# Moving the reload of a staging slot one store later on the GpSimd queue, in a one-core transformer and state-space kernel

## The chip, the core and the metric

The kernel runs on one core of a Trainium2 chip. A core has a matrix engine (TensorE, PE in the rows, with its weight loads as PEld), a vector engine (VectorE, DVE), an activation engine (ScalarE, ACT), GpSimd (POOL) and SyncE (SP). Each works through its own list of instructions in order and waits on semaphores for the others. Data moves between DRAM and the on-chip buffers by DMA; here SP, ACT and POOL issue DMAs. The metric is device time in microseconds (us) of one execution; lower is better.

## The reference

Two blocks run one after the other on 512 tokens of width 1024. Block one: an attention layer (eight stick-breaking heads, four differential heads), its output projection `w_o`, and a gated feed-forward. Block two: a wide input projection, a convolution branch, a bidirectional state-space scan, and 16 experts.

```python
x = x + mix @ w_o[layer]
h2 = rmsnorm(x, ffn_norm_g[layer])
x = x + (jax.nn.silu(h2 @ w_gate[layer]) * (h2 @ w_up[layer])) @ w_down[layer]
...
u = rms_norm(h, w_norm_mix[l])
proj = jnp.einsum('btd,dk->btk', u, w_in[l])
```

The change lies in the part of the program that covers these lines.

## The kernel before

Dense products of block one's feed-forward and of block two's projection are split products. A weight tile is written as a high part (a copy in the type `fp32r`, made by ACT) and a low part (tile minus high part, made by VectorE), and TensorE multiplies high by high, high by low and low by high.

The feed-forward has 76 such pieces. `FFT` is 22 (tiles of the hidden width), and the first 44 pieces are gate and up, two for each `m`; the other 32 are the down product, four for each of eight output tiles. `ffn_high(p)` (line 1314 and on) lets ACT make the high part of piece p in one of three buffers `WF`, as soon as TensorE has used piece p - 3; `ffn_low(p)` is VectorE's half of it. SP loads the raw weights into two slots of `ring`: 2 MB each for gate and up, 1.4 MB each for down, each issued when TensorE has finished the piece that last reads the slot.

Beside the feed-forward the kernel prepares the **72 weight tiles of the next projection** (`N_PROJ`, 512 KB each): their low parts are computed now and stored in DRAM, to be loaded again in the projection. Each tile q goes through a pipeline of four steps on three staging slots (`STAGE = 3`):

- POOL loads the raw tile into slot q % 3 of `arena` (`pre_load`, line 2303; DMA at line 2307, semaphore `pre_in`).
- ACT copies it as high part (`pre_high`, line 1328; instruction at line 1336). The high part goes to banks 6 and 7 of PSUM, of which there is one copy, so tile q waits for the low part of q - 1. The first `N_PRE_WO` tiles use `WF` instead, which is free until the feed-forward starts.
- VectorE subtracts and writes the low part to `PREL`, also three slots (`pre_low`, line 1854; instruction at line 1858).
- POOL stores it (line 2314, semaphore `pre_out`), after which both slots are free for tile q + 3.

Three tables say how many tiles are handled where in the lists of ACT and VectorE: `PRE_WO` for the eight output tiles of `w_o`, `PRE_GATE` for the 22 hidden tiles, `PRE_DOWN` for the eight output tiles of down. In the gate stage one tile of each `m` stands after `hidden_high(m - 1)` and the rest after `ffn_high(2m + 4)`; in the down stage they stand behind the four `ffn_high` of an output tile, and the square of the residual (`square("n3", ...)`) behind them. TensorE waits for the last of the 72 (`pe.wait_ge(S("pre_low"), N_PROJ)`) before the norm of the projection's input.

POOL's list here is one loop over q: wait for low part q, issue store q, and for q from 1 to 69 issue the load of tile q + 2, which needs store q - 1 to have landed.

Of the kernel before, what the change touches and what calls it, by code (L numbers as in the profile page):

```python
# [23 lines left out]
F32, F32R, U32 = mybir.dt.float32, mybir.dt.float32r, mybir.dt.uint32  # L24
# [15 lines left out]
FFT = FF // P  # L40
# [18 lines left out]
FBUF = 3  # L59
# [39 lines left out]
N_PROJ = len(PROJ)  # L99
STAGE = 3  # L100
PAIRS = 4
PRE_WO = [1, 2, 1, 2, 0, 0, 0, 0]
PRE_GATE = [2] * FFT
PRE_DOWN = [4, 3, 3, 3, 3, 3, 3, 0]
N_PRE_WO = sum(PRE_WO)
assert N_PRE_WO + sum(PRE_GATE) + sum(PRE_DOWN) == N_PROJ
FFN_W = 24
PROJ_W = FFN_W + 2 * FFT + 32
TAIL_W = PROJ_W + N_PROJ
# [33 lines left out]
def program(nc, inp, out):  # L143
    ctx = ExitStack()
    with ctx:
# [5 lines left out]
        def S(name):  # L151

            if name not in sems:
                sems[name] = ctx.enter_context(nc.semaphore(name))
            return sems[name]
# [19 lines left out]
        WF = ffn.enter_context(nc.sbuf_tensor("WF", [P, FBUF, PIECE], F32R))  # L175
# [60 lines left out]
        PS = ctx.enter_context(nc.psum_tensor("PS", [P, 8, 512], F32))  # L236
# [42 lines left out]


        _, ZSP, QK, V, MIX, ROPE = area([(P,), (5, 1280), (16, SEQ), (QB, D), (DT, SEQ), (2, SEQ)])

        SUMMED = U[:, 4, 0:3 * P]
# [43 lines left out]
        def pre_raw(q):  # L327
            return arena[:, PRE_AT + q % STAGE * PIECE:PRE_AT + q % STAGE * PIECE + PIECE]

        def pre_high_place(q):  # L330
            return PS[:, 6:8, :].rearrange("p a n -> p (a n)").bitcast(F32R) if q >= N_PRE_WO else WF[:, q % FBUF, :]

        def pair_of(p):
            return (p + 2) % PAIRS
# [49 lines left out]
        for b in range(2):  # L384
            block("out", (b,), (DT, 512))
        N_DENSE = len(loads)
        where = {name: n for n, (name, *_) in enumerate(loads)}

        slot_of, turn_, tail_turn = [], 0, 0
# [9 lines left out]
        for n, (name, *_) in enumerate(loads):  # L399
            count[slot_of[n]] += 16  # L400
            landed[name] = count[slot_of[n]]
# [90 lines left out]
        def freed(tag):  # L492
            b, n = order[tag]
            return S(f"freed{b}"), n

        def got(eng, tag):
            eng.wait_ge(*filled(tag))

        def free(ins, tag):
            return ins.then_inc(S(f"freed{order[tag][0]}"), 1)  # L500
# [657 lines left out]
        def _(act):  # L1158
# [3 lines left out]
            def square(nm, k, src, acc, T):  # L1162

                if k >= 3:
                    act.wait_ge(S("squares_added"), ADDS[nm] + k - 2)
                A(acc[:, 0:T] if k == 0 else SQ[:, k % 2, 0:T], src, ACT.Square).then_inc(S("sq_ready"), 1)
# [9 lines left out]
            def x_high(nm, k):  # L1176

                A(UX[:, 0, k, :], H[:, k, META:T2], ACT.Copy, scale=pcol(nm, k)).then_inc(S("x_high"), 1)
# [57 lines left out]
            for p in range(24):  # L1236
# [4 lines left out]
                if p - 2 in ROPE_AT:  # L1241
                    q = ROPE_AT.index(p - 2)
                    rope_root(2 * q)
                    rope_root(2 * q + 1)
                if p in ROPE_AT:
                    q = ROPE_AT.index(p)
# [19 lines left out]
            for n in range(DIFF_HEADS * QB + 3):  # L1266
# [14 lines left out]
                if 1 <= n <= DIFF_HEADS * QB:  # L1281
                    m = n - 1
# [6 lines left out]
                if n >= 3:  # L1289
                    m = n - 3  # L1290
# [23 lines left out]
            def ffn_high(p):  # L1314

                name = pieces[p][0]
                act.wait_ge(S(f"ring{slot_of[where[name]]}"), landed[name])
                if p >= FBUF:
                    act.wait_ge(*piece_used[p - FBUF])
                A(split_high(p), raw(p), ACT.Copy).then_inc(S("weights_high"), 1)  # L1320
# [7 lines left out]
            def pre_high(n):  # L1328

                for q in range(pre_turn[0], pre_turn[0] + n):  # L1330
                    act.wait_ge(S(f"pre_in{q % STAGE}"), 16 * (q // STAGE + 1))
                    if q >= N_PRE_WO:
                        act.wait_ge(S("pre_low"), q)
                    elif q >= FBUF:
                        act.wait_ge(S("pre_low"), q - FBUF + 1)
                    A(pre_high_place(q), pre_raw(q), ACT.Copy).then_inc(S("pre_high"), 1)  # L1336
                pre_turn[0] += n

            act.wait_ge(S("mix_ready"), DIFF_HEADS)
            for m in range(DT):  # L1340
                act.wait_ge(*freed(("wo", m)))
                x_high("ffn_g", m)
                square("n2", m, H[:, m, META:T2], RS, SEQ)
                pre_high(PRE_WO[m])
                if m == DT - FBUF - 1:
                    act.wait_ge(S("pre_low"), N_PRE_WO)
                if m >= DT - FBUF - 1 and m < DT - 1:
                    ffn_high(m - (DT - FBUF - 1))
            inverse_root("n2", (6,), SEQ)
            nc.scalar.preload_act_table_set("silu_and_others")  # L1350
            for m in range(FFT):
                ffn_high(2 * m + 3)
                if m >= 1:
                    hidden_high(m - 1)
                    pre_high(1)
                act.wait_ge(*freed(("ga", m)))
                A(SQ[:, m % 2, 0:SEQ], SQ[:, m % 2, 0:SEQ], ACT.Silu).then_inc(S("silu_ready"), 1)
                ffn_high(2 * m + 4)
                pre_high(PRE_GATE[m] - (m >= 1))
            nc.scalar.preload_act_table_set("natural_log_exp_and_others")  # L1360
# [342 lines left out]
        def _(dve):  # L1703
# [13 lines left out]
            def x_low(nm, k, base):  # L1717

                dve.wait_ge(S("x_high"), base + k + 1)
                V_.scalar_tensor_tensor(UX[:, 1, k, :], H[:, k, META:T2], pcol(nm, k), UX[:, 0, k, :].bitcast(F32), MUL, SUB)\  # L1720
                    .then_inc(S("x_low"), 1)

            def add_square(nm, k, acc, T):

                dve.wait_ge(S("sq_ready"), ADDS[nm] // (DT - 1) * DT + k + 1)
                if k >= 2:
                    dve.wait_ge(S("squares_added"), ADDS[nm] + k - 1)
                V_.tensor_tensor(acc[:, 0:T], acc[:, 0:T], SQ[:, k % 2, 0:T], ADD).then_inc(S("squares_added"), 1)
# [22 lines left out]
            for p in range(24):  # L1751
                b, m = divmod(p, 4)
# [19 lines left out]
                if p - 3 in ROPE_AT[:2]:  # L1772
                    q = ROPE_AT.index(p - 3)
# [34 lines left out]
            for n in range(DIFF_HEADS * QB + 2):  # L1808
# [11 lines left out]
                if n >= 2:  # L1820
                    m = n - 2
# [8 lines left out]
                if 1 <= n <= DIFF_HEADS * QB:  # L1830
                    m = n - 1
# [12 lines left out]
            def ffn_low(p):  # L1844
                dve.wait_ge(S("weights_high"), FFN_W + p + 1)
                V_.tensor_tensor(split_low(p), raw(p), split_high(p).bitcast(F32), SUB).then_inc(S("weights_low"), 1)  # L1846

            def hidden_low(m):
                dve.wait_ge(S("x_high"), GX_X + m + 1)
                V_.tensor_tensor(GX[:, 1, m, :], GXL[:, m, :], GX[:, 0, m, :].bitcast(F32), SUB).then_inc(S("x_low"), 1)  # L1850
# [3 lines left out]
            def pre_low(n):  # L1854

                for q in range(pre_turn[0], pre_turn[0] + n):
                    dve.wait_ge(S("pre_high"), q + 1)
                    V_.tensor_tensor(PREL[:, q % STAGE, :], pre_raw(q), pre_high_place(q).bitcast(F32), SUB).then_inc(S("pre_low"), 1)  # L1858
                pre_turn[0] += n

            for m in range(DT + 1):
                if m < DT:
                    got(dve, ("wo", m))
                    free(V_.tensor_tensor(H[:, m, META:T2], H[:, m, META:T2], PS[:, m % 4, :], ADD), ("wo", m))
                    dve.wait_ge(*freed(("wo", m)))
                if m >= 1:
                    x_low("ffn_g", m - 1, DT)
                    if m >= 2:
                        add_square("n2", m - 1, RS, SEQ)
                    pre_low(PRE_WO[m - 1])  # L1870
                if DT - FBUF <= m < DT:
                    ffn_low(m - (DT - FBUF))
            for m in range(FFT):
# [13 lines left out]
                ffn_low(2 * m + 4)  # L1887
                pre_low(PRE_GATE[m] - (m >= 1))
            hidden_low(FFT - 1)
# [105 lines left out]
            for g in range(GROUPS):  # L1995
# [18 lines left out]
                for s, c in enumerate(range(NC - 1, 0, -1)):  # L2014
                    t0, n = CHUNKS[c]
# [252 lines left out]
        def _(pool):  # L2268
# [34 lines left out]
            def pre_load(q):  # L2303

                if q >= STAGE:
                    pool.wait_ge(S(f"pre_out{q % STAGE}"), 16 * (q // STAGE))
                pool.dma_start(pre_raw(q), inp["w_proj"][q]).then_inc(S(f"pre_in{q % STAGE}"), 16)
# [4 lines left out]
            for q in range(N_PROJ):  # L2312
                pool.wait_ge(S("pre_low"), q + 1)
                pool.dma_start(low_dram[q], PREL[:, q % STAGE, :].bitcast(F32)).then_inc(S(f"pre_out{q % STAGE}"), 16)
                if 1 <= q <= N_PROJ - STAGE:
                    pre_load(q + STAGE - 1)

            pool.wait_ge(S("h_summed"), DT)
            pool.dma_start(h_dram, H[:, :, :]).then_inc(S("h_moved"), 16)
# [40 lines left out]
            for g in range(GROUPS):  # L2360
# [3 lines left out]
                for s, c in enumerate(range(NC - 1, 0, -1)):  # L2364
                    n = CHUNKS[c][1]
# [279 lines left out]
```

## Time and profile before

| | |
|---|---|
| median of 3 runs | 2706.44 us (2705.46 to 2711.19) |
| profiled execution, its own time | 2706.44 us |
| its span, first to last instruction | 2704.7 us |
| mean granted TensorE clock, share of full | 0.964 |
| PE busy | 2535.9 us (94%) |
| DVE busy / ACT busy / POOL busy | 1121.5 / 814.0 / 335.5 us |

The profile is one execution. Busy time counts what an engine executes; issuing a DMA is not counted as busy on the page, but a row of the timeline gives how long the issue took. In a timeline row the two numbers are start and duration, and the bracket says how long the engine was idle before it and who released it. For a DMA the profile knows the time from its issue to its landing. The stretch with which the change deals lies between 310 and 746 us of the span: the `w_o` product to 354.4 us, gate and up to 602.4 us, down to 726.2 us, then a norm and the start of block two's projection.

### The profile page before, as it was taken

What the parts mean: (1) busy time and instruction counts of PE and PEld (TensorE: products, weight loads), DVE (VectorE), ACT (ScalarE), POOL (GpSimd) and SP (SyncE); (2) the same over time, 40 slices, a digit from 0 to 9 for tenths busy, and PEclk for the clock granted to TensorE, in tenths of its full rate; (3) what the DMA queues carried; (4) which work ended last, traced back from release to release, by engine and by line L of the source; (5) the groups of instructions that cost most, each with busy time, mean ns of one, the idle gap of its engine ahead of it and who ended that gap; (6) DMA issues with size and microseconds to landing.
All of it is one profiled execution on the core that took longest, in us unless ns stands there. A gap on an engine that the chain in (4) does not pass through costs nothing.

```text
span 2704.7 us, 42580 instructions
## 1 busy us (share of the span) xinstructions
PE 2535.9 (94%) x18335; PEld 1583.1 (59%) x18335; DVE 1121.5 (41%) x1530; ACT 814.0 (30%) x1347; POOL 335.5 (12%) x411
## 2 busy tenths in 40 slices
PE   8998999999799898989779998999999999999996
PEld 6754478887589797979569973333333333333332
DVE  4336466653538878796965332111111111111111
ACT  3256454443345454544453221000000010000001
POOL 0033012111201212121520000000000000000000
PEclk9999999999989998999779999999999999999998
DMA  5100268885745454546432259999999999999993
GB/s 207 63 32 1 82 230 296 285 284 210 276 164 198 124 196 125 193 123 203 112 142 72 85 208 352 410 398 409 395 398 399 393 396 395 397 395 397 395 403 129
DMA packets 128630, 674.20 MB, mean 249 GB/s; under 512 B 19236, under 2 KB 52004, under 8 KB 99140
## 3 DMA queue, kind: packets, MB, share of 16 engines
q1 hardware_dynamic: 55584, 552.65, 52.5%
q0 software_dynamic: 25632, 88.49, 9.8%
q10 hardware_dynamic: 47236, 30.42, 4.1%
q8 instruction: 145, 2.38, 0.3%
q14 instruction: 33, 0.27, 0.0%
HBM read 617.47 MB, written 54.04 MB: 248 GB/s over the span
## 4 chain that ended last, share of the span: by engine, by line
PE 80%; DVE 12%; DMA 4%; ACT 2%; issue 2%; POOL 1%; ACTq 0%; POOLq 0%; DVEq 0%; SPq 0%
PE PS L1111 37%; PE PS L811 11%; PE PS L1013 4%; DVE H L1977 4%; PE PS L757 3%; PE PS L753 3%; PE PS L754 3%; DMA arena<-w_proj 2%; PE PS L1018 2%; PE PS L657 1%; PE PS L604 1%; PE PS L605 1%; PE PS L608 1%; PE PS L728 1%; PE PS L1101 1%
## 5 line engine op out<-in xcount | busy, mean ns | idle before, releaser
L1111 PE MATMUL PS<-expert_ring_low,U 128*32 128x512 f32 x4608 | 508.4, 593 | 0.9 <-DVE U L2219 0.9
L1111 PE MATMUL PS<-expert_ring_high,U 128*32 128x512 f32 x4608 | 504.8, 592 | 0.0
L811 PE MATMUL PS<-XH,RINGF 128*128 128x264 f32 x2304 | 400.0, 292 | 1.2 <-ACT arena L1428 1.2
L1111 PEld LDWEIGHTS PS<-expert_ring_high,U 128*32 128x32 f32 x4608 | 148.2, 110 | 336.7 <-issue 335.7
L1111 PEld LDWEIGHTS PS<-expert_ring_low,U 128*32 128x32 f32 x4608 | 146.4, 110 | 331.3 <-issue 330.3
L811 PEld LDWEIGHTS PS<-XH,RINGF 128*128 128x128 f32 x2304 | 331.2, 193 | 9.6 <-issue 6.8
L811 PE MATMUL PS<-UH,RINGF 128*128 128x264 f32 x1152 | 238.8, 290 | 0.0
L2231 DVE TENSOR_TENSOR H<-H,PS 128x512 f32<-128x512 f32 x32 | 22.0, 688 | 438.3 <-PE PS L1111 422.8
L1977 DVE SCALAR_TENSOR_TENSOR H<-arena,par,H 128x528 f32<-128x528 f32 x240 | 198.2, 871 | 1.4
L811 PEld LDWEIGHTS PS<-UH,RINGF 128*128 128x128 f32 x1152 | 184.9, 195 | 0.0
L1674 ACT ACTIVATE H<-PS 128x512 f32<-128x512 f32 x32 | 19.1, 597 | 456.5 <-PE PS L1111 456.5
L2414 POOL DMA_INDIRECT residual_rows<-H,scatter_rows x16 | 25.1, 1571 | 928.8 <-DVE H L2245 928.8
L753 PE MATMUL PS<-UX,WF 128*128 128x512 f32 x352 | 138.5, 393 | 1.2 <-DVE UX L1720 1.2
L754 PE MATMUL PS<-UX,WF 128*128 128x512 f32 x352 | 137.1, 389 | 0.0
L1858 DVE TENSOR_TENSOR PREL<-arena,PS 128x1024 fp32r<-128x1024 f32 x66 | 80.5, 1220 | 90.9 <-ACT PS L1336 90.2
L2007 DVE SCALAR_TENSOR_TENSOR SQ<-arena,par,SQ 128x528 f32<-128x528 f32 x144 | 109.7, 766 | 6.4 <-ACT SQ L1416 3.7
L1320 ACT ACTIVATE WF<-ring 128x1024 fp32r<-128x1024 f32 (+1 forms) x76 | 70.7, 943 | 107.7 <-PE PS L757 104.3
L1846 DVE TENSOR_TENSOR RINGF<-ring,WF 128x1024 fp32r<-128x1024 f32 (+1 forms) x76 | 81.4, 1083 | 44.3 <-ACT WF L1320 44.2
L1336 ACT ACTIVATE PS<-arena 128x1024 fp32r<-128x1024 f32 x66 | 67.7, 1025 | 105.3 <-DMA arena<-w_proj 102.1
L1685 ACT ACTIVATE SQ<-PS 2x512 f32<-2x512 f32 x32 | 18.9, 591 | 260.6 <-PE PS L1111 260.2
L1483 ACT ACTIVATE ring<-ring 128x128 f32<-128x128 f32 (+1 forms) x320 | 89.3, 368 | 14.9 <-POOL ring L2355 14.7
L2237 DVE COPY U<-PS 128x256 f32<-128x256 f32 x32 | 13.6, 425 | 191.1 <-PE PS L1105 191.1
(352 smaller groups left out, 3661.2 us busy)
## 6 DMA issues: line engine op xcount, KB each, us to landing
expert_ring_low<-w_experts SPq DMA_DIRECT2D x96, 2048.0 KB, 11.6
expert_ring_high<-w_experts SPq DMA_DIRECT2D x96, 2048.0 KB, 11.4
arena<-w_proj POOLq DMA_DIRECT2D x72, 512.0 KB, 5.3
projection_low_parts<-PREL POOLq DMA_DIRECT2D x72, 512.0 KB, 4.2
ring<-w_proj SPq DMA_DIRECT2D x72, 512.0 KB, 3.7
RINGF<-projection_low_parts SPq DMA_DIRECT2D x72, 512.0 KB, 4.6
ring<-w_gu SPq DMA_DIRECT2D x11, 2048.0 KB, 9.4
ring<-ssd_sums ACTq DMA_DIRECT2D x32, 512.0 KB, 8.1
```

Of the source, the lines that this page charges most:

```text
L753: nc.tensor.matmul(PS[:, bank, :], hi[:, k, :], src[:, 0, k0 + k, :], start=(start and k == 0), stop=False)
L754: nc.tensor.matmul(PS[:, bank, :], hi[:, k, :], src[:, 1, k0 + k, :], start=False, stop=False)
L757: last = nc.tensor.matmul(PS[:, bank, :], lo[:, k, :], src[:, 0, k0 + k, :], start=False, stop=(stop and k == n - 1))
L811: last = nc.tensor.matmul(PS[:, banks[i], 0:HT], w[:, k, :], x[:, k, lo:hi], start=start, stop=stop)
L1013: nc.tensor.matmul(PS[:, banks[i], 0:HT], wh[:, k, :], x(k)[:, lo:hi], start=(first and k == 0 and x is high), stop=False)
L1111: mm = nc.tensor.matmul(PS[QUAD * t:QUAD * t + QUAD, bank, :], stat(t), move(t), start=start, stop=stop)
L1320: A(split_high(p), raw(p), ACT.Copy).then_inc(S("weights_high"), 1)
L1483: ins = A(FR[i % 2][d][0:n, h, 0:n], FR[i % 2][d][0:n, h, 0:n], ACT.Exp, bias=FT[0:n, c, j:j + 1])
L1846: V_.tensor_tensor(split_low(p), raw(p), split_high(p).bitcast(F32), SUB).then_inc(S("weights_low"), 1)
L1858: V_.tensor_tensor(PREL[:, q % STAGE, :], pre_raw(q), pre_high_place(q).bitcast(F32), SUB).then_inc(S("pre_low"), 1)
L1977: ins = V_.scalar_tensor_tensor(acc, CP[:, u % 3, j:j + T2], par[:, w0 + j:w0 + j + 1], acc, MUL, ADD)
L2007: V_.scalar_tensor_tensor(co, xp[:, k:k + T2], par[:, w0 + k:w0 + k + 1], co, MUL, ADD)\
```

## The change

The loop of POOL now loads tile q + 3 behind store q, for every q for which there is one, instead of tile q + 2. The semaphore on which `pre_load` waits is computed from the tile, so the load behind store q now waits for store q itself. Beside it the tables change: three tiles instead of six in the `w_o` stage (one each at m = 1, 2 and 3), and three instead of two at m = 5, 11 and 17 of the gate stage. The down stage keeps its 22. With three tiles in the first stage no buffer of `WF` is used twice there, and the wait for that goes.

```diff
-PRE_WO = [1, 2, 1, 2, 0, 0, 0, 0]
-PRE_GATE = [2] * FFT
+PRE_WO = (1, 2, 3)
+PRE_GATE = [2 + (m in (5, 11, 17)) for m in range(FFT)]
 PRE_DOWN = [4, 3, 3, 3, 3, 3, 3, 0]
-N_PRE_WO = sum(PRE_WO)
-assert N_PRE_WO + sum(PRE_GATE) + sum(PRE_DOWN) == N_PROJ
+assert len(PRE_WO) + sum(PRE_GATE) + sum(PRE_DOWN) == N_PROJ
...
-                    if q >= N_PRE_WO:
+                    if q >= len(PRE_WO):
                         act.wait_ge(S("pre_low"), q)
-                    elif q >= FBUF:
-                        act.wait_ge(S("pre_low"), q - FBUF + 1)
                     A(pre_high_place(q), pre_raw(q), ACT.Copy).then_inc(S("pre_high"), 1)
...
-                pre_high(PRE_WO[m])
+                if m in PRE_WO:
+                    pre_high(1)
...
-                    pre_low(PRE_WO[m - 1])
+                    if m - 1 in PRE_WO:
+                        pre_low(1)
...
             for q in range(N_PROJ):
                 pool.wait_ge(S("pre_low"), q + 1)
                 pool.dma_start(low_dram[q], PREL[:, q % STAGE, :].bitcast(F32)).then_inc(S(f"pre_out{q % STAGE}"), 16)
-                if 1 <= q <= N_PROJ - STAGE:
-                    pre_load(q + STAGE - 1)
+                if q + STAGE < N_PROJ:
+                    pre_load(q + STAGE)
```

POOL's list at the start of its loop, before (`pre_out0` counts the landed stores of tiles 0, 3, 6 and so on, `pre_out1` those of 1, 4, 7):

```order
L2307 DMA arena<-w_proj 128x1024 x2
L2314 DMA projection_low_parts<-PREL 128x1024 [waits pre_low] x2
L2307 DMA arena<-w_proj 128x1024 [waits pre_out0]
L2314 DMA projection_low_parts<-PREL 128x1024 [waits pre_low]
L2307 DMA arena<-w_proj 128x1024 [waits pre_out1]
L2314 DMA projection_low_parts<-PREL 128x1024 [waits pre_low]
L2307 DMA arena<-w_proj 128x1024 [waits pre_out2]
```

The same place after:

```order
L2306 DMA arena<-w_proj 128x1024 x2
L2313 DMA projection_low_parts<-PREL 128x1024 [waits pre_low]
L2306 DMA arena<-w_proj 128x1024 [waits pre_out0]
L2313 DMA projection_low_parts<-PREL 128x1024 [waits pre_low]
L2306 DMA arena<-w_proj 128x1024 [waits pre_out1]
L2313 DMA projection_low_parts<-PREL 128x1024 [waits pre_low]
L2306 DMA arena<-w_proj 128x1024 [waits pre_out2]
```

Before, two stores precede the load that waits for the first of them; after, each load waits for the store right in front of it. The whole list has the same instructions, with three stores instead of two in a row at its end.

ACT's list in the `w_o` stage, output tiles m = 0 to 3, before (UX is the high part of the input, the square goes to RS or SQ, WF<-arena is a prepared tile):

```order
L1178 ACTIVATE UX<-H,par 128x512
L1166 ACTIVATE RS<-H 128x512
L1336 ACTIVATE WF<-arena 128x1024
L1178 ACTIVATE UX<-H,par 128x512
L1166 ACTIVATE SQ<-H 128x512
L1336 ACTIVATE WF<-arena 128x1024 x2
L1178 ACTIVATE UX<-H,par 128x512
L1166 ACTIVATE SQ<-H 128x512
L1336 ACTIVATE WF<-arena 128x1024
```

And after:

```order
L1177 ACTIVATE UX<-H,par 128x512
L1165 ACTIVATE RS<-H 128x512
L1177 ACTIVATE UX<-H,par 128x512
L1165 ACTIVATE SQ<-H 128x512
L1333 ACTIVATE WF<-arena 128x1024
L1177 ACTIVATE UX<-H,par 128x512
L1165 ACTIVATE SQ<-H 128x512
L1333 ACTIVATE WF<-arena 128x1024
```

Output tile 0 has no prepared tile any more, and tile 1 has one instead of two.

## Rows read from the trace of the kernel before

**Rows 1.** The page: the chain that ended last, by engine.

```profile
PE 80%; DVE 12%; DMA 4%; ACT 2%; issue 2%; POOL 1%; ACTq 0%; POOLq 0%; DVEq 0%; SPq 0%
```

**Rows 2.** Busy time by stretch; then granted clock, DMA share, GB/s.

```profile
354.40:602.40 248.00, 246.75 (x1078) 202.07 (x1077) 151.09 (x162) 118.59 (x139) 45.89 (x87) 1.00 0.79 274
602.40:726.20 123.80, 119.55 (x512) 96.19 (x510) 55.81 (x62) 42.86 (x53) 19.65 (x38) 0.99 0.71 252
726.20:744.40 18.20, 0.01 (x1) 0.00 (x0) 10.93 (x14) 5.06 (x7) 3.70 (x7) 0.65 0.60 215
```

**Rows 3.** Waits from 354 to 746 us: total us, times, longest.

```profile
ACT PS L1336 <- DMA arena<-w_proj: 102.1, 44, 5.8
...
POOL arena L2307 <- DMA projection_low_parts<-PREL: 40.6, 13, 6.8
...
PE PS L554 <- DVE U L1728: 18.2, 1, 18.2
```

**Rows 4.** Timeline of PE: end of `w_o`, and the norm behind down.

```profile
310.17 44.80 PE L728 MATMUL PS<-arena,ring 128*128 128x512 f32 x104
...
744.45 2.10 PE L554 MATMUL PS<-U,consts_sb 128*128 128x264 f32 x4 [18.24 <-DVE U L1728]
```

**Rows 5.** The chain in order of time, at the end of the down stage.

```profile
729.55 1.04 ACT PS L1336
...
732.65 4.65 DMA arena<-w_proj
...
737.32 1.04 ACT PS L1336
```

**Rows 6.** Timeline of POOL: stores (L2314) and loads (L2307).

```profile
372.21 0.53 POOL L2314 DMA_DIRECT2D projection_low_parts<-PREL  x1 [21.52 <-DVE PREL L1858]
...
636.05 0.53 POOL L2314 DMA_DIRECT2D projection_low_parts<-PREL  x1 [33.06 <-DVE PREL L1858]
...
639.21 0.54 POOL L2307 DMA_DIRECT2D arena<-w_proj  x1 [0.25 <-DMA projection_low_parts<-PREL]
```

**Rows 7.** Single DMAs issued at 391.36, 394.89, 372.73 and 374.58 us.

```profile
arena<-w_proj POOLq DMA_DIRECT2D x1, 512.0 KB, 3.9
...
projection_low_parts<-PREL POOLq DMA_DIRECT2D x1, 512.0 KB, 2.9
...
arena<-w_proj POOLq DMA_DIRECT2D x1, 512.0 KB, 5.2
...
projection_low_parts<-PREL POOLq DMA_DIRECT2D x1, 512.0 KB, 4.6
```

**Rows 8.** DMAs issued from 370 to 600 us, then from 630 to 745.

```profile
ring<-w_gu SPq DMA_DIRECT2D x9, 2048.0 KB, 9.8
ring<-w_down SPq DMA_DIRECT2D x2, 1408.0 KB, 8.7
...
ring<-w_down SPq DMA_DIRECT2D x4, 1408.0 KB, 8.0
```

**Rows 9.** Single DMAs issued at 402.64, 403.17 and 406.46 us.

```profile
projection_low_parts<-PREL POOLq DMA_DIRECT2D x1, 512.0 KB, 9.1
arena<-w_proj POOLq DMA_DIRECT2D x1, 512.0 KB, 9.8
...
projection_low_parts<-PREL POOLq DMA_DIRECT2D x1, 512.0 KB, 7.8
```

**Rows 10.** Timelines of ACT and PE at the end of the gate stage.

```profile
599.37 1.01 ACT L1336 ACTIVATE PS<-arena 128x1024 fp32r<-128x1024 f32 x1
...
602.74 0.74 ACT L1320 ACTIVATE WF<-ring 128x640 fp32r<-128x640 f32 x1 [0.41 <-PE PS L757]
...
610.00 0.39 PE L753 MATMUL PS<-GX,WF 128*128 128x512 f32 x1
```

**Rows 11.** Timeline of PE behind its longest wait in the down stage.

```profile
646.23 0.79 PE L753 MATMUL PS<-GX,WF 128*128 128x512 f32 x1 [2.54 <-ACT WF L1320]
646.82 0.63 PE L754 MATMUL PS<-GX,WF 128*128 128x512 f32 x1
```

More of the change, by code:

```diff
@@ L330, in pre_high_place @@
         def pre_high_place(q):
-            return PS[:, 6:8, :].rearrange("p a n -> p (a n)").bitcast(F32R) if q >= N_PRE_WO else WF[:, q % FBUF, :]
+            return PS[:, 6:8, :].rearrange("p a n -> p (a n)").bitcast(F32R) if q >= len(PRE_WO) else WF[:, q, :]
         def pair_of(p):
@@ L1343, in _ @@
                 square("n2", m, H[:, m, META:T2], RS, SEQ)
-                pre_high(PRE_WO[m])
+                if m in PRE_WO:
+                    pre_high(1)
                 if m == DT - FBUF - 1:
-                    act.wait_ge(S("pre_low"), N_PRE_WO)
+                    act.wait_ge(S("pre_low"), len(PRE_WO))
                 if m >= DT - FBUF - 1 and m < DT - 1:
```

## The prediction

> **What bounds the kernel now.** I read the chain by engine first, then the stretches of the stage that changes, then its waits, then single rows of the GpSimd queue. The chain lies on TensorE for 80% of the span [rows 1]. In the gate and up stretch it has no gap worth naming: 246.75 us busy of 248.00 [rows 2]. In the down stretch it is idle 4.25 us of 123.80, and behind down 18.2 us in which it does nothing [rows 2]; that wait stands before the norm [rows 3, 4]. What it waits for is the last of the 72 prepared tiles: the chain there alternates between the load of a raw tile (4.65 us) and ACT's copy of it, and the last copy starts at 737.32 us [rows 5]. So the preparation is hidden under gate and up, and is late by some microseconds at the end of down. ACT waits for raw tiles 102.1 us in all, but never more than 5.8 us at once [rows 3]; TensorE, whose pieces are three buffers ahead, feels little of it. The change therefore counts only by the pace at which prepared tiles come: two tiles per 10.96 us in the gate stage (248 us over 22 and the start), and as fast as possible in the down stage. Everything behind 746 us is left as it is, and a shift of this stage goes through to the end.
>
> **The new pace of POOL.** Before, a load waits for a store issued one tile earlier, so POOL was held up by landings for only 40.6 us, 13 times [rows 3], and two loads are on their way beside two stores. In the quiet end of down a tile came every 3.9 us (two copies 7.77 us apart, 729.55 and 737.32, with one between them) [rows 5]. After the change POOL issues store q, stands until that same store has landed, issues load q + 3, and only then looks at store q + 1. If low part q + 1 is already there, which it is once POOL is the late one, one tile costs POOL:
> - issue of the load, 0.53 us [rows 6];
> - the store's time from issue to landing;
> - landing to next issue, about 0.3 us (the store of 636.05 landed 2.9 us later, at 638.95, and the load went out at 639.21) [rows 6].
>
> How long the store takes is the disputed number, because now it is issued 0.53 us behind a load. Alone, a load lands in 3.9 us and a store in 2.9 [rows 7]. The load issued at 372.73 landed at 377.93, the store issued at 374.58 behind it at 379.18, 1.25 us after the load; it took 4.6 us [rows 7]. I take this: load landing at 3.9, store 1.25 later at 5.15 us, next load at 5.43. The ends are 3.7 us a tile (0.53 + 2.9 + 0.3, a store that does not notice the load) and 5.8 (the load at 4.3 instead of 3.9, a third of the way to the 5.2 seen). The row behind a load is the nearest, so 5.43.
>
> The Trainium skill, "DMA: Bandwidth & Descriptors", section "Queues, rings and completion order", says that an engine consumes descriptors in ring order and that a semaphore increment lands only after every earlier write of that DMA engine. By that rule a store issued right behind a load cannot report before the load's writes; the trace agrees with its 1.25 us [rows 7].
>
> **Big loads of SP.** Each 2 MB or 1.4 MB load of SP takes 8 to 10 us to land [rows 8], and what POOL has on its way then lands only behind it: stores took 9.1 and 7.8 us, the load between them 9.8 [rows 9]. Three POOL transfers were caught there; after the change it is two. A pair caught in full would land at about 9 and 10.3 us instead of 3.9 and 5.15, so it costs 5 to 5.5 us; a load that gets through just before (SP's load issued in the second half of a cycle) leaves 3 to 4. I take 4, ends 3 and 5.5. There are 9 + 2 of them in the gate stage, 4 in down, and one group of the projection's first loads near 711 us, which I count as a fifth [rows 8].
>
> **Gate stage.** The first store goes out at 372.2 as before [rows 6], its load at 375.4. Tile 49, the last of this stage (3 + 47 tiles, as 6 + 44 before), is 43 cycles later: 43 x 5.43 = 233.5, plus 11 x 4 = 44, gives 652.9, landed at 656.8. Before, ACT copied it at 599.37; the next high part was ready at 603.5 and TensorE needed it at 610.0 [rows 10], a slack of 6.5 us. 656.8 - 599.4 - 6.5 = **51 us** later. Ends: 43 x 4.8 + 33 gives 13 us; 5.43 with 5.5 for a big load gives 67.
>
> **Down stage.** The first eight pieces prepare nothing, so POOL catches up and three raw tiles lie ready, one more than before. From the first store (636.05) and its load (639.2) to the load of tile 71 it is 18 cycles: 97.7, plus 5 x 4 = 20, landed at 760.8 in the clock of before. Then it was at 737.32 [rows 5]: **23.5 us** later. Ends: 7 (4.8 us a cycle, 3 for a big load) and 31. TensorE's own waits of 4.25 us lie inside this.
>
> **The tables.** Three tiles fewer in the `w_o` stage save ACT three copies of about 1 us and VectorE three of 1.2 us, but TensorE runs that product without a gap (44.80 us, 104 matmuls) [rows 4]: nothing, between -1 and 0 us. Three tiles more in the gate stage are counted above; alone, at 5.43 each, they are 16 of the 51 us, and in the rhythm of before they would have been hidden. The removed wait for `WF` held nothing up: 0.
>
> **Sum.** 51 + 23.5 = 74.5 us on the profiled execution's own 2706.44 us (span 2704.7, 1.7 us around it), which is also the median: **2781 us**. Low ends 13 + 7 = 20 give 2726; high ends 67 + 31 = 98 give 2805.
>
> **Rivals.**
> - *The store runs beside the load.* It lands with it, at 3.9, and a cycle is 4.2 us. Gate: 375.4 + 43 x 4.2 + 44 + 3.9 = 603.9, late by 4.5, less than the slack, 0. Down: 639.2 + 75.6 + 20 + 3.9 = 738.7, +1.4 us. Time 2708. For it: the rate of 274 GB/s over the stretch leaves room [rows 2]. Against it: the 4.6 us of the store behind a load. The Trainium skill, same page, section "Anatomy of one DMA — SWDGE (gpsimd) path", prices a DMA at about 2.0 us plus bytes over 436 GB/s whatever is ahead of it, an estimate of 3.2 us here; a cycle would then be 4.0 us and the sum about 0 to -2. The 4.6 us speaks against that rule too.
> - *Faster: the third staged tile wins.* Stores stay at 2.9 us everywhere and a cycle is 3.7 us, below the 3.9 at which tiles came before, which is the point from which it decides. The last six tiles start at 716 with three ready: copies and low parts 2.3 us apart, stores at 718.6, 722.3 and 726.0, loads 3.2 us behind each, the last at 729.2, landed at 733.1 against 737.3, so -4.2. Of TensorE's 4.25 us of waits the first (2.54) depends on the fourth tile of the burst and stays, 1.7 go. Sum -6: 2700. Against it the same 4.6.
> - *Heavier: the clock.* After a wait of 2.54 us TensorE's matmuls stood 0.43 us apart instead of 0.23 for about 3.4 us (starts 646.82 and on) [rows 11], the lower of its two levels, 1.6 us lost each time. With waits of some 2 to 5 us once per two `m` I expect it hidden, since POOL sets the pace. If it is not, 11 times 1.6, 18 us more: 2799.
>
> **How the numbers follow.** Forecast 0.72 with its own range 2726 to 2805, heavier 0.13, store beside load 0.09, faster 0.06. The range given is 2726 to 2812, the heavier case's spread on top. A difference below 0.2% (5.4 us) can't be told from none with this kernel. Slower by more: 0.72 + 0.13 = 0.85; within: 0.09; faster: 0.06.
>
> **What the changed profile would show.** POOL's loads wait for landed stores some 65 times instead of 13, for 200 us and more in sum. Stores behind a load take about 4.6 us when no big load runs. ACT's copies wait for raw tiles in single waits well over 5.8 us, TensorE waits for ACT's high parts from about 430 us on, first short, then several us twice per 22 us, and the gate stretch is about 300 us long. Down ends near 800 and the norm still waits for the last tile by some 20 us. Nothing behind it changes length. If stores behind a load take 3.4 us or less, the forecast falls to the first rival; if TensorE shows no waits in the gate stretch, the pace argument is wrong altogether. If the low clock stands in many slices and ACT no longer waits for loads, TensorE and not POOL has become the bound.

## The result, and the profile after

| | before | after |
|---|---|---|
| median of 4 runs | 2705.95 us (2703.19 to 2711.19) | **2822.53 us** (2817.68 to 2826.47) |
| profiled execution, its own time | 2706.44 us | 2812.78 us |
| its span | 2704.7 us | 2811.0 us |
| mean granted TensorE clock | 0.964 | 0.953 |

The changed kernel is slower: ratio 1.0428, 95% interval 1.0405 to 1.045. The forecast was 2781 us with a range of 2726 to 2812. The sign was right, and the size was too small by 41 us against the median, which lies 10 us above the range, or by 32 against the profiled execution.

The chain of the changed kernel by engine, from the page, against [rows 1]:

```profile
PE 69%; DMA 14%; DVE 11%; issue 2%; ACT 2%; POOL 2%; ACTq 0%; POOLq 0%; DVEq 0%; SPq 0%
```

The DMA's share rose from 4 to 14%. The same chain from 354 to 866 us, by line, lies for 72.5% on stores of low parts:

```profile
by line: DMA projection_low_parts<-PREL 72.5%; POOL arena L2306 6.0%; issue 5.1%; PE PS L752 3.0%; PE PS L756 3.0%; PE PS L753 2.9%; DMA arena<-w_proj 1.8%; PE PS L797 1.6%; ACT PS L1333 0.6%; PE PS L553 0.6%; DVE PREL L1856 0.5%; DVE U L17
```

Read it as store, POOL's next load issue, store, and so on. This is one serial loop, with TensorE beside it.

Busy time by stretch, in the columns of [rows 2]; the stages are gate and up, down, and the wait before the norm:

```profile
354.40:681.50 327.10, 274.03 (x1077) 217.27 (x1076) 148.87 (x161) 115.92 (x138) 46.98 (x89) 0.91 0.64 213
681.50:822.95 141.45, 123.40 (x512) 98.97 (x511) 55.62 (x63) 44.44 (x54) 19.02 (x36) 0.95 0.65 216
822.95:853.28 30.33, 0.00 (x1) 0.03 (x1) 12.42 (x15) 6.52 (x8) 5.82 (x11) 0.57 0.57 176
```

Against [rows 2], gate and up grew from 248.0 to 327.1 us, down from 123.8 to 141.5, and the wait from 18.2 to 30.3. That is 79 + 18 + 12 = 109 us. The rate in the gate stage fell from 274 to 213 GB/s: the same transfers moved faster before, so the rate that the loop reaches is not the most that the DMA engines gave in this stage.

Waits from 354 to 870 us (total us, times, longest), against [rows 3]:

```profile
POOL arena L2306 <- DMA projection_low_parts<-PREL: 381.0, 66, 10.0
ACT PS L1333 <- DMA arena<-w_proj: 268.2, 60, 8.7
DVE PREL L1856 <- ACT PS L1333: 239.4, 63, 7.6
...
PE PS L752 <- ACT WF L1319: 64.5, 20, 6.2
...
PE PS L553 <- DVE U L1726: 30.3, 1, 30.3
```

Read it from the top down. POOL waits for stores 66 times instead of 13. ACT therefore waits for raw tiles, VectorE for ACT's copy, and TensorE for high parts of the feed-forward, which stand behind the prepared tiles' copies in ACT's list. The row of TensorE and ACT, 64.5 us in 20 waits, has no counterpart of this size before: there TensorE waited for high parts four times, 4.2 us in all, and only in the down stage.

### The profile page after: what moved, and what is told of

It reads as the page before. It is cut to its first block, busy times and chain, and to the rows that moved or that the text cites. A ratio compares the mean times of both kernels' runs of the same rounds, so it can differ in the third digit from the quotient of the medians.

```text
span 2811.0 us, 42580 instructions
## 1 busy us (share of the span) xinstructions
PE 2564.1 (91%) x18335; PEld 1596.4 (57%) x18335; DVE 1116.9 (40%) x1530; ACT 812.5 (29%) x1347; POOL 336.8 (12%) x411
## 4 chain that ended last, share of the span: by engine, by line
PE 69%; DMA 14%; DVE 11%; issue 2%; ACT 2%; POOL 2%; ACTq 0%; POOLq 0%; DVEq 0%; SPq 0%
PE PS L1110 35%; DMA projection_low_parts<-PREL 13%; PE PS L810 10%; PE PS L1012 4%; DVE H L1976 4%; PE PS L1017 2%; PE PS L727 2%; PE PS L656 1%; PE PS L603 1%; PE PS L604 1%; POOL arena L2306 1%; PE PS L607 1%; PE PS L1100 1%; PE PS L752 1%; PE PS L756 1%
## 5 line engine op out<-in xcount | busy, mean ns | idle before, releaser
L752 PE MATMUL PS<-UX,WF 128*128 128x512 f32 x352 | 152.6, 433 | 47.2 <-ACT WF L1319 46.4
L753 PE MATMUL PS<-UX,WF 128*128 128x512 f32 x352 | 148.8, 423 | 0.0
L752 PEld LDWEIGHTS PS<-UX,WF 128*128 128x128 f32 x352 | 73.8, 210 | 71.4 <-issue 53.7
L752 PE MATMUL PS<-GX,WF 128*128 128x512 f32 x176 | 73.7, 419 | 23.9 <-ACT WF L1319 18.0
L2306 POOL DMA_DIRECT2D arena<-w_proj x72 | 38.3, 532 | 468.1 <-DMA projection_low_parts<-PREL 400.1
## 6 DMA issues: line engine op xcount, KB each, us to landing
expert_ring_high<-w_experts SPq DMA_DIRECT2D x96, 2048.0 KB, 11.4
```

The costliest lines, as they stand in the source:

```text
L752: nc.tensor.matmul(PS[:, bank, :], hi[:, k, :], src[:, 0, k0 + k, :], start=(start and k == 0), stop=False)
L753: nc.tensor.matmul(PS[:, bank, :], hi[:, k, :], src[:, 1, k0 + k, :], start=False, stop=False)
```

## Three cycles of the loop, up close

POOL's timeline of the changed kernel in a stretch without a large load, and then into one (start, duration, idle before and releaser):

```profile
531.85 0.53 POOL L2306 DMA_DIRECT2D arena<-w_proj  x1 [4.89 <-DMA projection_low_parts<-PREL]
532.37 0.54 POOL L2313 DMA_DIRECT2D projection_low_parts<-PREL  x1
538.02 0.53 POOL L2306 DMA_DIRECT2D arena<-w_proj  x1 [5.11 <-DMA projection_low_parts<-PREL]
...
544.10 0.53 POOL L2306 DMA_DIRECT2D arena<-w_proj  x1 [5.02 <-DMA projection_low_parts<-PREL]
...
550.53 0.53 POOL L2306 DMA_DIRECT2D arena<-w_proj  x1 [5.38 <-DMA projection_low_parts<-PREL]
551.05 0.54 POOL L2313 DMA_DIRECT2D projection_low_parts<-PREL  x1
561.03 0.53 POOL L2306 DMA_DIRECT2D arena<-w_proj  x1 [9.45 <-DMA projection_low_parts<-PREL]
```

The DMAs issued at 531.85 and 532.37 us:

```profile
arena<-w_proj POOLq DMA_DIRECT2D x1, 512.0 KB, 4.7
projection_low_parts<-PREL POOLq DMA_DIRECT2D x1, 512.0 KB, 5.4
```

A quiet cycle is 6.17 us (531.85 to 538.02). The load lands after 4.7 us, at 536.5. The store, issued 0.52 later, lands at 537.8, some 1.2 us behind the load, and the next load goes out about 0.25 us after that. The last cycle shown met one of SP's 2 MB loads and took 10.5 us. Counted here and below are 61 cycles: 43 from the load of tile 6 to that of tile 49, for the gate stage, and 18 from tile 53 to tile 71, for down. Their median is 6.2 us, and 19 are longer than 6.8.

## The experiments

Theory A is the prediction's: POOL's wait for the landing of the store in front of it sets a serial cycle per tile, and the loop's move brings this, not the tables. Each kernel was timed in turn with the kernel before on one chip, and each ratio is against that.

**The loop alone (e1)** and **the tables alone (e2).** The first has the tables of before and the new loop; the second has the new tables and the old loop.

Edit of e1, against the kernel before:

```diff
-                if 1 <= q <= N_PROJ - STAGE:
-                    pre_load(q + STAGE - 1)
+                if q + STAGE < N_PROJ:
+                    pre_load(q + STAGE)
```

Edit of e2, against the changed kernel:

```diff
-                if q + STAGE < N_PROJ:
-                    pre_load(q + STAGE)
+                if 1 <= q <= N_PROJ - STAGE:
+                    pre_load(q + STAGE - 1)
```

> The tables of the kernel before with the changed loop of POOL (load of tile q + 3 behind store q). Theory A, POOL's wait for the store it has just issued: the quiet cycle of 6.1 us per tile is the same as in the changed kernel, but the gate stage has 40 cycles to its last load instead of 43, 20 us less, of which some 4 us are lost again in the w_o stage, where six tiles must now pass POOL; time 2706 + 100 = about 2806. Theory B, the tables carry a good part of the loss: the time falls to 2760 or less.

> The new tables with the loop of before (load of tile q + 2 behind store q). Theory A: 0 to +5 us, 2706 to 2711, TensorE waits at most a few us around hidden tiles 5, 11 and 17, where five tiles fall in 22 us. Theory B (tables): +40 us or more.

e1: 2801.86 us against 2708.72, ratio 1.0339 [1.0316, 1.0363]; about 2806 was expected. e2: 2717.22, ratio 1.0026 [1.0015, 1.0038]. The loop carries 93 us by itself, so theory A's main part stands. The tables cost some 7 to 9 us by themselves (the ratio and the medians), which I had put at 0 to 5. Waits in e2 from 354 us on:

```profile
POOL arena L2306 <- DMA projection_low_parts<-PREL: 60.6, 18, 7.6
PE PS L553 <- DVE U L1726: 18.6, 1, 18.6
...
PE PS L752 <- ACT WF L1319: 13.1, 9, 2.9
```

The wait before the norm is as long as before (18.6 against 18.2 in [rows 3]), but TensorE now waits 13.1 us for high parts, nine times: 5.6 us in the gate stage, where it had no such wait before, and 7.5 in the down stage, where it had 4.2. The norm starts at 754.65 us instead of 744.45. The gate stage now takes 47 tiles (3 x 3 + 19 x 2), not 44. That the old loop doesn't deliver these in time fits the waits, but no run separates it from the tables' other half, the three tiles fewer in the `w_o` stage.

**The wait on the consumer (e3, e4).** Same instructions, same three slots, same dependence. The wait for the stored low part stands on VectorE, just before it overwrites the slot of `PREL`, and no longer on POOL before it loads. The load itself needs only the raw tile's slot, which VectorE has read when `pre_low` counts q + 1, and POOL has waited for that already. e3 has the new tables, e4 those of before.

```diff
                     dve.wait_ge(S("pre_high"), q + 1)
+                    if q >= STAGE:
+                        dve.wait_ge(S(f"pre_out{q % STAGE}"), 16 * (q // STAGE))
...
-                if q >= STAGE:
-                    pool.wait_ge(S(f"pre_out{q % STAGE}"), 16 * (q // STAGE))
                 pool.dma_start(pre_raw(q), inp["w_proj"][q]).then_inc(S(f"pre_in{q % STAGE}"), 16)
```

> The changed kernel, but the wait for store q moves from POOL, ahead of the load of tile q + 3, to VectorE, ahead of its writing low part q + 3; POOL issues store q and load q + 3 in one go and never waits for a landing. Everything else, the table and the early order of loads too, is as changed. Theory A: the whole loss goes and the third staged tile pays: the last six tiles of down need no landing of a store, loads go out at 718.6, 721 and 723.3 in the clock of before, the last copy starts near 729 instead of 737, TensorE's waits of 4 us in down mostly go; 2695, between 2688 and 2702. Theory C, the order of a load ahead of the next store on the shared rings costs by itself (loads 4.6 instead of 3.9 us, stores 5.3 instead of 2.9): a good part of the loss stays, 2740 or more.

> As the kernel with the wait on VectorE, but with the tables of the kernel before. Theory A: 2695 as there, within 3 us of it, since the tables are worth nothing once tiles come in time. Theory B: more than 10 us between the two.

e3: 2690.47 us, ratio 0.9933 [0.9912, 0.9954]. e4: 2689.53, ratio 0.9931 [0.9912, 0.995]. About 2695 was expected of both. With the wait on POOL this loop costs 93 us or more; with the same wait on VectorE it gains 18 to 19. Nothing of the loss stays, so theory C's 2740 is out, although a load still stands beside each store. The two differ by 0.9 us, so the tables are worth nothing once tiles come in time. POOL in e4, where the load leaves directly behind its store:

```profile
504.24 0.54 POOL L2314 DMA_DIRECT2D projection_low_parts<-PREL  x1 [4.00 <-DVE PREL L1860]
504.77 0.53 POOL L2307 DMA_DIRECT2D arena<-w_proj  x1
510.15 0.54 POOL L2314 DMA_DIRECT2D projection_low_parts<-PREL  x1 [4.85 <-DVE PREL L1860]
510.68 0.53 POOL L2307 DMA_DIRECT2D arena<-w_proj  x1
```

And what is left of the waits in e4:

```profile
DVE PREL L1860 <- ACT PS L1336: 22.3, 17, 2.5
...
PE PS L554 <- DVE U L1728: 10.8, 1, 10.8
...
ACT PS L1336 <- DMA arena<-w_proj: 10.8, 5, 2.7
```

From the gate stage on POOL's stores wait for VectorE only, ACT hardly waits for tiles (10.8 us against 102.1 in [rows 3]), and no wait of TensorE for a high part is left in either stage. VectorE, which now has the wait for the landed store, is not seen to wait for one.

**Is TensorE, or its clock, the bound? (e6)** One of the three products of each feed-forward piece is left out (the high part of the weight by the low part of the input); all else stays.

```diff
-                    nc.tensor.matmul(PS[:, bank, :], hi[:, k, :], src[:, 1, k0 + k, :], start=False, stop=False)
```

> The changed kernel without the product of high weights by low input in all 76 pieces of the feed-forward (a third of their matmuls left out, so the feed-forward is computed less precisely): a gate piece takes 3.66 us instead of 5.48, a down piece 2.5 instead of 3.76, 120 us less work for TensorE. Theory A, POOL's cycle sets the pace of gate, up and down: only the first eight down pieces, in which no tile is prepared, get shorter, 10 us; 2812, and not below 2800. Theory F, TensorE with its low clock behind each wait is the bound of the changed kernel: 2740 or less.

2810.11 us, ratio 1.037 [1.0352, 1.0387]. Waits in e6:

```profile
POOL arena L2305 <- DMA projection_low_parts<-PREL: 390.1, 66, 11.0
...
PE PS L752 <- ACT WF L1318: 151.2, 37, 11.4
```

A third of the feed-forward's matmuls is gone, and the time falls by 7 to 12 us against the changed kernel's two medians; 10 were expected, from the first eight down pieces, which prepare nothing. The trace has them there: from the load of tile 52 to that of tile 53 it is 8.9 us instead of 20.7. The cycles themselves did not get shorter (43 in the gate stage took 308.7 us, in the changed kernel 304.6). TensorE's waits for ACT more than doubled, from 64.5 to 151.2 us, while POOL's stayed (390.1 against 381.0). The rival "heavier", by which the low clock was to add to the loop's pace, had no place: outside those eight pieces TensorE has time left.

**What sets the cycle's length? (e5, e8)** Theory D: load and store, issued half a microsecond apart, slow each other. e5 stores half of each low part, and the projection reads that half twice. e8 makes POOL wait for the load as well before it issues the next store, so that each has the queue to itself.

Edit of e5, at the store:

```diff
-                pool.dma_start(low_dram[q], PREL[:, q % STAGE, :].bitcast(F32)).then_inc(S(f"pre_out{q % STAGE}"), 16)
+                pool.dma_start(low_dram[q][:, 0:PIECE // 2], PREL[:, q % STAGE, 0:PIECE // 2].bitcast(F32)).then_inc(S(f"pre_out{q % STAGE}"), 16)
```

Edit of e8:

```diff
                 if q + STAGE < N_PROJ:
                     pre_load(q + STAGE)
+                    pool.wait_ge(S(f"pre_in{q % STAGE}"), 16 * (q // STAGE + 2))
```

> The changed kernel with stores of half a tile, 256 KB instead of 512; the projection reads that half twice (the low parts it uses are wrong in their second half, so part of the computation is left out). Theory D, the 6.1 us of a quiet cycle are bytes of a load and a store on the same 16 DMA engines: a store behind a load lands 0.6 us sooner and the load gains a few tenths, cycle 5.4 to 5.5, over 61 cycles 37 us less, 2785. Theory E, the cycle is made of fixed delays of a landing and the size of the store is nothing: 2815 to 2825 as the changed kernel.

> The changed kernel in which POOL also waits until load q + 3 has landed before it looks at the next store, so that loads and stores of the prepared tiles never run together. If the 6.1 us are two transfers slowing each other (4.6 and 5.3 us against 3.9 and 2.9 alone), loads land in 3.9 and stores in 2.9 again and a quiet cycle is 3.9 + 0.3 + 2.9 + 0.3 = 7.4 us, 1.3 more than the changed kernel, 61 times: +79, about 2900. If other traffic of this stage slows them (theory G), loads stay at 4.5 or above and the cycle is 8.5 or more: 2960.

e5: 2760.19 us, ratio 1.0188 [1.0169, 1.0207], below what either theory gave. The quiet cycle is 5.43 us, as theory D said, but that is 0.77 less in each of 61 cycles, 47 us and not 37, and the mean cycle of the gate stage fell a little more still, from 7.08 to 6.22 us. Of the 62 us to the changed kernel's first median (57 to its second) the cycles give 48; the profiled executions are 49 apart. e8: 2910.03 us, ratio 1.0748 [1.0727, 1.0769]. Its quiet cycle is theory D's 7.4 us. What goes beyond the +79 it expected comes from cycles that meet a big load: 61 cycles took 522.2 us instead of 427.6, and some 73 of these 95 us are the quiet cycle's 1.2. Two loads of e5 on POOL, and the two DMAs between them:

```profile
512.89 0.53 POOL L2306 DMA_DIRECT2D arena<-w_proj  x1 [4.02 <-DMA projection_low_parts<-PREL]
...
518.31 0.53 POOL L2306 DMA_DIRECT2D arena<-w_proj  x1 [4.36 <-DMA projection_low_parts<-PREL]
```
```profile
arena<-w_proj POOLq DMA_DIRECT2D x1, 512.0 KB, 4.5
projection_low_parts<-PREL POOLq DMA_DIRECT2D x1, 256.0 KB, 4.6
```

The same in e8, where one follows the other:

```profile
508.13 0.53 POOL L2306 DMA_DIRECT2D arena<-w_proj  x1 [5.79 <-DMA projection_low_parts<-PREL]
512.39 0.54 POOL L2313 DMA_DIRECT2D projection_low_parts<-PREL  x1 [3.73 <-DMA arena<-w_proj]
515.54 0.53 POOL L2306 DMA_DIRECT2D arena<-w_proj  x1 [2.62 <-DMA projection_low_parts<-PREL]
```
```profile
arena<-w_proj POOLq DMA_DIRECT2D x1, 512.0 KB, 4.0
projection_low_parts<-PREL POOLq DMA_DIRECT2D x1, 512.0 KB, 2.9
```

The next table has the cycles without a big load, for landings the middle eight tenths of them:

| store behind the load | load lands after | store lands after | cycle, median of the gate stage |
|---|---|---|---|
| none until the load has landed (e8) | 3.7 to 4.0 | 2.9 | 7.39 |
| 256 KB (e5) | 4.3 to 4.6 | 4.4 to 4.7 | 5.43 |
| 512 KB (after) | 4.4 to 4.7 | 5.2 to 5.5 | 6.2 |

Theory D holds for this order, with the load first. Alone the two take 3.9 and 2.9 us, as before in [rows 7], but with the store behind the load both are longer. Even the half store does not report ahead of the load issued before it: it lands at 513.41 + 4.6 = 518.0, the load at 512.89 + 4.5 = 517.4. In the changed kernel the store lands 1.26 us after its load (median of 64 pairs, least 1.22), in e5 0.65 us (least 0.53): half the bytes, half the distance.

With the store first it is another matter. The two DMAs of e4 issued at 504.24 and 504.77 us, the store and the load shown above:

```profile
projection_low_parts<-PREL POOLq DMA_DIRECT2D x1, 512.0 KB, 2.9
arena<-w_proj POOLq DMA_DIRECT2D x1, 512.0 KB, 4.6
```

The store is as fast as alone, and only the load behind it is longer. The same holds wherever such a store goes out with nothing of POOL's in flight: 2.9 us in all four cases of the kernel before and all six of e7, and at most 3.0 in nine of e4's eleven. So a load ahead makes the store take 5.4 us, and a load behind does not.

**An order that goes further (e7).** e4 with three tiles of the down stage moved into gate and up:

```diff
-PRE_GATE = [2] * FFT
-PRE_DOWN = [4, 3, 3, 3, 3, 3, 3, 0]
+PRE_GATE = [2 + (m in (5, 11, 17)) for m in range(FFT)]
+PRE_DOWN = [4, 3, 3, 3, 3, 3, 0, 0]
```

> The kernel with the wait on VectorE and the old tables, and three tiles moved from down output tile 6 to m = 5, 11 and 17 of the gate stage, so that nothing is prepared behind the last but two output tiles. The gate stage has room once POOL does not wait (TensorE did not wait there with 47 tiles). The wait before the norm was 10.9 us and falls to some 4, the part that is the last output tile's own sums: 6 to 7 us less than 2689.5, 2683. Rival: the gate's third tile or VectorE's new wait brings waits of TensorE, and it is the same or slower.

2685.64 us against 2683 expected, ratio 0.9917 [0.99, 0.9933]: the lowest median of the study, though its interval overlaps e4's. Its wait before the norm:

```profile
PE PS L554 <- DVE U L1728: 3.6, 1, 3.6
```

**Repetitions (r1, r2, r3)**: the changed kernel, e4 and e7 again, on another chip.

> The changed kernel once more, for a second profile: the first profiled execution (2812.8 us) lay 10 us under the median of the others. If the difference is chance in how POOL's cycles meet SP's big loads, the second profile differs in the sum of the caught cycles and not in the quiet cycle (6.2 us) nor outside 370 to 860 us; the median is 2815 to 2825. If profiling itself makes the kernel faster, this profiled run is again the lowest by 5 us or more.

> For comparison with the next kernel on one chip: 2689 to 2692 us, ratio to the kernel before 0.993.

> The wait before the norm is 7.2 us shorter than in the kernel beside it by the profiles; if nothing is given back, 2683 to 2685, 6 to 7 us under it. If it is given back in the gate stage or in the projection behind, within 3 us of it.

r1: 2817.37 us, ratio 1.0394 [1.038, 1.0408]. r2: 2690.48, 0.9936 [0.9921, 0.995]. r3: 2686.8, 0.9919 [0.9906, 0.9932]. In the first comparison the changed kernel's profiled execution (2812.78) lay below all four timed ones, in r1 it was the highest of all (2824.19), so it isn't the profiling that shortens it. In r1 the quiet cycle was 6.22 us again, the long cycles' excess over it summed to 56.1 us instead of 52.0, and the norm began at 859.10 instead of 853.28. This gives about 6 of the 11 us between the two. The other 5 arise behind the norm, which had not been expected. They are of the size of chance: from the norm's start to the end it is 1957 to 1964 us in the profiles of all thirteen runs, the kernel before among them (1960), and the two of the changed kernel are 1958 and 1963. Why this part varies stays open. The norm's start is therefore the cleaner measure of the stage, free of these 6 us.

## Why the sign was right and the size wrong

The terms, in order of the prediction; positions are those of the profiled executions.

- *What bounds the stage, and the serial cycle*: right. POOL's 66 waits were forecast as some 65, and e1, e3 and e6 show that the loop carries the loss, that the wait's place on POOL does it, and that TensorE is not the bound.
- *The quiet cycle*: **this step failed.** It read "load landing at 3.9, store 1.25 later at 5.15 us, next load at 5.43". The 1.25 holds (1.26 measured), though its row was a store issued 1.85 us behind the load and not 0.5, and so do the 0.53 and the 0.3. The 3.9 does not: I took the time of a load with nothing beside it for a load that now always has a store half a microsecond behind it, and such a load takes 4.6. No load of the kernel before has this neighbour. The rows at hand with a neighbour at all were the 5.2 of [rows 7] and the 4.65 of [rows 5], each with a store issued half a microsecond ahead of the load (at 372.21 and at 732.12 us). With 4.65 the sum would be 4.65 + 1.25 + 0.28 = 6.18, and 6.2 is what came; since that row has the other order, the agreement is partly luck. 0.77 us in 43 cycles is 33 us, more than the whole miss of the gate stage.
- *Big loads*: 4 us each, 44 in the gate stage. From the load of tile 6 at 374.90 to that of tile 49 at 679.47 it is 304.6 us; less 43 x 6.2 there remain 38, or 3.5 for each of 11. The term was 6 us too high.
- *Gate stage*: forecast 51, measured by the first store of the down stage 79.3 (636.05 to 715.36). The 28.3 between are 33.1 for the cycle, -6 for the big loads, 0.6 for the later landing, 1.1 for a slack of 5.4 us instead of 6.5, and -0.5 at the start. The start and the 5.4 are fitted from the positions: tile 49's copy begins 31.3 us before the first store of down, and did 36.7 us before it in the kernel before. The end of the range, 67, had the cycle at 5.43 and only the big load at its worst, and the low end had a cycle of 4.8 us that is derived nowhere. My own upper bound of 5.8 us for the cycle stood in the text and was not carried into the range; with it the gate end would have been 67 + 43 x 0.37 = 83 us, and the measured 79 inside.
- *Down stage*: forecast 23.5, measured 108.8 - 79.3 = 29.5 (last load 732.65 to 841.50). 18 cycles took 123.0 us against 117.7: 18 x 6.2 and 11.4 for the big loads instead of 20.
- *The tables*: forecast nothing beside the cycles. e2 shows 7 to 9 us where the loop is the old one. In the changed kernel they are about 2817 to 2823 less 2802, so 15 to 20 us by the medians. I had said 16, as a part of the 51, and that in the old rhythm they would have been hidden; that half was wrong. The 16 is not confirmed as three more cycles either: against e1 the norm starts 8.8 us later in the changed kernel's first profile and 14.6 in r1, and the first store of down 5.7 and 10.2 us later. e1's cycles in the gate stage were longer (7.46 us in the mean from tile 9 on, against 7.05), for a reason that no run shows.
- *Behind the stage*: nothing was forecast; 108.8 us at the norm became 106.3 of span.
- *Sum*: 28.3 + 6.0 - 2.5 = 31.8 us, the whole distance from 2781 to 2812.78. The rest up to the first median, 10 us, is spread between executions; the -2.5 lies within the spread behind the norm.

The rivals: a store that runs beside its load without cost would have needed stores that land after some 3.4 us, and a third staged tile that wins would have needed 2.9; 5.4 was measured. "Heavier" came near in time (2799) and was wrong in cause, by e6. The low clock itself is there: the gate stage's granted clock is 0.91 of full speed against 1.00 [rows 2], and behind a wait the matmuls of the changed kernel start some 0.45 us apart instead of 0.23, as the prediction read behind [rows 11]:

```profile
656.40 0.66 PE L752 MATMUL PS<-UX,WF 128*128 128x512 f32 x1 [2.21 <-ACT WF L1319]
656.86 0.63 PE L753 MATMUL PS<-UX,WF 128*128 128x512 f32 x1
```

But TensorE waits for pieces anyway, and e6 shows that what it loses so is hidden.

The signs that the prediction named: TensorE's first wait for a high part came at 437.79 us (forecast from about 430), ACT's longest wait for a tile is 8.7 us (over 5.8). The gate stretch is 327 us long where about 300 was said, down ends at 823 instead of near 800, the norm's wait is 30 us and not some 20, and stores behind a load take 5.4 us, not 4.6.

## What to carry to other kernels

Put the wait for a slot's release on the engine that next writes the slot, not on the queue that issues the transfers: an in-order queue that waits for its own last transfer can start nothing else meanwhile, and its cycle is a full landing. When such a cycle is added up from a trace, take each duration from a transfer that has the same neighbours, ahead and behind, as in the new order, and carry the worst of each step into the range. Where stages hide one another, leave out part of the cover (here a third of the matmuls), since a time that hardly moves tells which of them is the bound.

## What was not expected of the hardware

- **Of two transfers on one queue the second is longer, and the first too if it is the load.** A 512 KB load takes 3.7 to 4.0 us alone and 4.4 to 4.7 with a store issued 0.5 us behind it; the store 2.9 alone, 5.2 to 5.5 there. A store with a load 0.5 us behind it keeps its 2.9. The pair still takes less than one after the other (6.2 against 7.39 us a cycle). The Trainium skill, "DMA: Bandwidth & Descriptors", section "Anatomy of one DMA — SWDGE (gpsimd) path", prices each at about 2.0 us plus bytes over 436 GB/s, by estimate 3.2 us for either; the runs show 2.9 for the store, 3.9 for the load, and 4.6 and 5.4 as a pair. The order in which a pair reports agrees with the Trainium skill, same page, section "Queues, rings and completion order", by which a semaphore increment lands only after every earlier write of the same DMA engine: in none of the 64 pairs of the changed kernel, nor in the 64 of e5 with half the size, does the store land before the load ahead of it.
- **A load to the chip is the slower one.** With equal bytes and none of POOL's transfers beside, the store to DRAM lands 1.0 us sooner than the load from it (medians 2.9 against 3.9 in e8).
- **Longer landings can do no harm.** In e7 the prepared tiles' loads take 7.1 us at the median from 370 to 680 us, more than the 4.6 of the changed kernel, and TensorE has no wait for a high part there: a load goes out every 5.6 us in the mean, often before the last has landed. Throughput per tile counts, not the latency of one:

```profile
arena<-w_proj POOLq DMA_DIRECT2D x57, 512.0 KB, 7.1
```

- **Open.** e7's wait before the norm is 7.2 us shorter than e4's, but its median is only 3.9 us lower (3.7 in the repetition, where within 3 or 6 to 7 was expected), with intervals that overlap. The stage itself keeps the gain: the norm starts 7.5 us earlier in e7's profile than in e4's (723.07 against 730.53) and 7.7 earlier in r3's than in r2's. That the medians show only half of it is within the spread of the part behind the norm; whether something there gives it back is not shown.
